# Output projection of three token tiles wholly in upper and lower parts, with three gate chunks converted later, on one Trainium2 core

## What is computed

```python
heads = concatenate([rms_norm(y_pool), rms_norm(y_attn), rms_norm(y_ssm)])
h = layer_norm(DN_ALPHA * x + heads @ w_out[i])
combine = route(h, w_router, router_bias)
ffn = moe(h, combine, ...)
ple = sigmoid(h @ w_ple_gate[i]) * (p[i] @ w_ple_proj[i])
x = layer_norm(DN_ALPHA * h + ffn + ple)
```

## Time and profile before

| | |
|---|---|
| time, median of 3 runs | 428.99 us (428.87 to 429.12) |
| time of the profiled execution | 429.05 us |
| its span, first to last instruction | 427.3 us |
| TensorE matmul busy | 413.3 us, 97% |
| TensorE weight load busy | 238.1 us, 56% |
| VectorE busy | 255.4 us, 60% |
| ScalarE busy | 129.6 us, 30% |
| GpSimd busy | 93.6 us, 22% |
| mean granted TensorE clock | 0.993 |

### The profile page before, as it was taken

The page is one execution under the profiler, slowest core; times in us unless marked ns, Lnnn a source line. Parts: engine busy times, 40 slices in busy tenths (PEclk is TensorE's granted clock), DMA queues, the critical chain, the costliest instruction groups (busy, mean ns, idle before and its releaser), DMA issues.

```text
span 427.3 us, 5594 instructions
## 1 busy us (share of the span) xinstructions
PE 413.3 (97%) x2167; PEld 238.1 (56%) x2167; DVE 255.4 (60%) x464; ACT 129.6 (30%) x235; POOL 93.6 (22%) x132
## 2 busy tenths in 40 slices
PE   8899999999999999999999999999999999999992
PEld 5677655469667555676577887333333433333271
DVE  2999985986873999998867524211101112224987
ACT  4721336025497890200621011011110111111243
POOL 2830269275000800000000742010111111000000
PEclk9999999999999999999999999999999999999997
DMA  7994103251997891111490428999999999977313
GB/s 264 431 397 129 49 2 66 68 130 51 276 411 295 285 392 63 49 49 51 158 384 8 191 43 325 425 410 413 418 417 418 421 411 411 423 289 247 152 45 153
DMA packets 33626, 102.76 MB, mean 240 GB/s; under 512 B 14882, under 2 KB 16082, under 8 KB 26816
## 3 DMA queue, kind: packets, MB, share of 16 engines
q1 hardware_dynamic: 26032, 92.79, 56.1%
q0 software_dynamic: 4016, 7.97, 5.6%
q10 hardware_dynamic: 3552, 1.65, 1.4%
HBM read 93.29 MB, written 15.24 MB: 254 GB/s over the span
## 4 chain that ended last, share of the span: by engine, by line
PE 67%; issue 23%; DVE 4%; DMA 3%; POOL 1%; ACT 1%; DVEq 0%; POOLq 0%; ACTq 0%
PE bank L1307 20%; PE bank L1317 10%; PE bank L952 7%; PE bank L1000 5%; PE bank L1302 3%; PE bank L967 3%; PE bank L992 3%; PE bank L1009 2%; PE bank L988 2%; PE bank L1067 2%; PE bank L1057 2%; POOL slot_scratch L595 1%; PE bank L995 1%; PE bank L1123 1%; PE bank L1122 1%
## 5 line engine op out<-in xcount | busy, mean ns | idle before, releaser
L1307 PE MATMUL bank<-region_a,region_g 128*64 128x512 f32 (+1 forms) x224 | 77.8, 594 | 0.0
L1317 PE MATMUL bank<-region_a,region_c 128*64 128x512 f32 (+1 forms) x160 | 43.7, 596 | 0.0
L1885 DVE TENSOR_TENSOR region_c<-region_c,bank 128x256 f32<-128x256 f32 x12 | 5.1, 421 | 64.6 <-ACT region_c L907 64.6
L1307 PE MATMUL bank<-region_h,region_g 128*64 128x512 f32 (+1 forms) x96 | 42.4, 594 | 0.0
L1307 PE MATMUL bank<-region_b,region_g 128*64 128x512 f32 (+1 forms) x96 | 42.4, 594 | 0.0
L1307 PE MATMUL bank<-region_c,region_g 128*32 128x512 f32 (+1 forms) x96 | 42.4, 594 | 0.0
L1878 DVE COPY region_g<-bank 128x512 f32<-128x512 f32 x24 | 15.5, 687 | 40.4 <-PE bank L1302 40.4
L1307 PEld LDWEIGHTS bank<-region_a,region_g 128*64 128x64 f32 (+1 forms) x224 | 22.2, 123 | 25.1 <-issue 24.4
L1151 PE MATMUL bank<-region_b,region_e 128*128 128x512 f32 x68 | 32.9, 607 | 0.0
L907 ACT ACTIVATE region_c<-bank 128x256 f32<-128x256 f32 x12 | 4.6, 384 | 83.9 <-PE bank L1307 83.9
L952 PE MATMUL bank<-region_e,region_a 128*128 128x512 f32 x64 | 28.0, 595 | 0.0
(11 more groups left out here) (364 smaller groups left out, 881.9 us busy)
## 6 DMA issues: line engine op xcount, KB each, us to landing
region_a<-in_w_exp_down SPq DMA_DIRECT2D x10, 1024.0 KB, 14.4
region_a<-in_w_exp_gate SPq DMA_DIRECT2D x7, 1024.0 KB, 8.4
region_a<-in_w_exp_up SPq DMA_DIRECT2D x7, 1024.0 KB, 12.1
region_b<-in_w_out SPq DMA_DIRECT2D x1, 4096.0 KB, 14.7
expert_scratch<-zero_scratch SPq DMA_DIRECT2D x8, 512.0 KB, 9.5
region_c<-in_w_ple_gate SPq DMA_DIRECT2D x2, 1536.0 KB, 23.1
region_b<-in_w_exp_gate SPq DMA_DIRECT2D x3, 1024.0 KB, 10.3
region_b<-in_w_exp_up SPq DMA_DIRECT2D x3, 1024.0 KB, 12.3
```

What stands on the lines that cost most here:

```text
L1307: return mm(out_[at:at + width].rearrange("p (u n) -> p u n", u=2), x[:, k, at:at + width], w[:, k], start=(k == 0), stop=(k == KD - 1), t ...
L1317: return mm(bank[banks[half]][at:at + width, :], act_e[:, r, 2, k * P + at:k * P + at + width], w[:, k, half * 512:half * 512 + 512], star ...
```

## The change

Tiles 1 to 3 of the output projection are multiplied in parts for all three groups. The upper parts of the heads' and weights' chunks 2, 3, 4 are made by ScalarE too (in new homes: among them the place of `pT`, and the place where the upper parts of gate chunks 4, 5, 6 will stand), the lower parts of the heads by VectorE, and the lower parts of weight chunks 2, 3, 4 by GpSimd, half by half, when tile 0 has read that half. The gate's chunks 7 and 3 are converted by ScalarE after the RMS square roots; chunks 4, 5, 6 (`PG_LAST`) by ScalarE once the last output product is done and ahead of the square root of tile 3, and by VectorE after `hidden_lower(3)` and ahead of the routing. `wo_read` goes up once per bank. `pT` is loaded after the last output product. A table load for the square root is placed by hand. The first gate products no longer wait for all chunks.

```diff
-WO_SPLIT = (5, 6, 7, 0, 1)
+WO_SPLIT = (5, 6, 7, 0, 1, 2, 3, 4)
-PG_FIRST, PG_ORDER = (0, 1, 2), (5, 6, 7, 4, 3)
+PG_FIRST, PG_NEXT, PG_LAST = (0, 1, 2), (7, 3), (4, 5, 6)
+PG_LATER = len(PG_NEXT + PG_LAST)
...
         wo_hi = {k: over(f"out_upper{k}", D, at) for k, at in
-                 ((0, A0), (1, A0 + 4 * D), (5, A0 + 4 * 2 * D), (6, A0 + 4 * 3 * D), (7, H0 + 4 * 6144))}
+                 ((0, A0), (1, A0 + 4 * D), (5, A0 + 4 * 2 * D), (6, A0 + 4 * 3 * D), (7, H0 + 4 * 6144),
+                  (2, A0 + 4 * 10240), (3, A0 + 4 * 11264), (4, A0 + 4 * 12288))}
...
+                  (2, H0 + 4 * 2048), (3, H0 + 4 * 2432), (4, H0 + 4 * 7168))}
...
             load(w_pp, io["w_ple_proj"].rearrange("(k p) n -> p k n", p=P), "wpp_in")
-            load(pT, io["pT"].rearrange("(k p) t -> p k t", p=P), "wpp_in")
...
                 sp.dma_start(h_d[t * P:(t + 1) * P, :], xh[:, t, :]).then_inc(S[f"h_out{t}"], 16)
 
             sp.wait_ge(S["pe_wo"], 2 * NT)
+            load(pT, io["pT"].rearrange("(k p) t -> p k t", p=P), "wpp_in")
             load_gu(0)
...
             add_squares(4, 2, 0)
+            for half in range(2):
+                cols = slice(half * 512, half * 512 + 512)
+                gp.wait_ge(S["wo_hi_set"], 16)
+                gp.wait_ge(S["pe_wo"], half + 1)
+                for k in MIX_AT[2]:
+                    g.tensor_tensor(wo_lo[k][:, cols], w_o[:, k, cols], wo_hi[k][:, cols], ALU.subtract).then_inc(S["gp_lo_set"], 1)
+            gp.wait_ge(S["pe_wo"], 2 * NT)
...
             for k in WO_SPLIT:
+                if k == 2:
+                    ac.wait_ge(S["pv_evac"], 3)
                 a.activation(hd_hi[k][:], hdT[:, k, P:T], ACT.Copy).then_inc(S["wo_hi_set"], 1)
             ac.wait_ge(S["wo_in"], 16)
-            for k in (0, 1, 5, 6, 7):
+            for k in (0, 1, 5, 6, 7, 2, 3, 4):
                 a.activation(wo_hi[k][:], w_o[:, k, :], ACT.Copy).then_inc(S["wo_hi_set"], 1)
...
-            ac.wait_ge(S["wpg_in"], 48)
-            for k in PG_ORDER[:4]:
-                gate_upper(k)
+            a.preload_act_table(ACT.Sqrt)
             ac.wait_ge(S["pe_sq"], 1)
...
+            ac.wait_ge(S["wpg_in"], 48)
             ac.wait_ge(S["sq_added"], 5)
-            gate_upper(PG_ORDER[4])
+            for k in PG_NEXT:
+                gate_upper(k)
...
             for t in range(NT):
+                if t == NT - 1:
+                    ac.wait_ge(S["pe_wo"], 2 * NT)
+                    for k in PG_LAST:
+                        gate_upper(k)
                 ac.wait_ge(S["z_ready"], t + 1)
...
                 for half in range(2):
-                    pe.wait_ge(S["wo_read"], 2 * t + half - 1)
-                    for group in range(2):
-                        if t == 1 and half == 0:
-                            pe.wait_ge(S["wo_hi_set"], (7, 10)[group])
-                            pe.wait_ge(S["wo_lo_set"], (7, 10)[group])
-                        mix_split(t, half, group)
-                    mix_part(t, half, 2).then_inc(S["pe_wo"], 1)
+                    for group in range(3):
+                        pe.wait_ge(S["wo_read"], 3 * (2 * t + half - 2) + group + 1)
+                        if t == 1:
+                            if group == 2:
+                                pe.wait_ge(S["wo_hi_set"], 16)
+                                pe.wait_ge(S["gp_lo_set"], 3 * half + 3)
+                            elif half == 0:
+                                pe.wait_ge(S["wo_hi_set"], (10, 13)[group])
+                                pe.wait_ge(S["wo_lo_set"], (10, 13)[group])
+                        last = mix_split(t, half, group)
+                    last.then_inc(S["pe_wo"], 1)
...
                 if half == 0:
-                    pe.wait_ge(S["ple_lo_set"], KD + t + 1)
+                    pe.wait_ge(S["ple_lo_set"], KD - len(PG_LAST) + t + 1)
+                elif t == 0:
+                    pe.wait_ge(S["ple_lo_set"], KD + NT)
...
+            ple_gate(0)
             pe.wait_ge(S["wpp_in"], 32)
-            ple_gate(0)
             ple_proj(0)
             turn_h(NT - 1)
...
                         last = stt(xh[:, t, cols], bank[WO_AT[half_][group]][:], rms_r[:, group, t:t + 1], xh[:, t, cols], ALU.mult, ALU.add)
-                        if group < 2:
-                            link(last)
-                    last.then_inc(S["wo_read"], 1)
-                    dv.wait_ge(S["wo_read"], 2 * t + half_ + 1)
+                        last.then_inc(S["wo_read"], 1)
+                        dv.wait_ge(S["wo_read"], 3 * (2 * t + half_) + group + 1)
...
                 if t == 0:
-                    gate_lower_of(1)
-                    gate_lower_of(2)
+                    dv.wait_ge(S["ple_hi_set"], 1)
+                    gate_lower(PG_NEXT[0])
                 elif t == 1:
-                    gate_lower_of(3)
                     hidden_lower(0)
                 elif t == 2:
-                    gate_lower_of(4)
+                    gate_lower(PG_NEXT[1])
             hidden_lower(1)
...
             hidden_lower(3)
+            for k in PG_LAST:
+                gate_lower(k)
```

More of the change, by code:

```diff
@@ L309, in trunk @@
             "kern_in kern_done rot_ready xrot_done "
-            "u_out u_back m0_in s_ready s_moved y_evac y_out y_back yin_ready gelu_done glu_lo_set glu_sig ssm_done "
+            "u_out u_back m0_in s_ready s_moved y_evac y_out gp_lo_set yin_ready gelu_done glu_lo_set glu_sig ssm_done "
             "pool_ready pool_mixed pe_u pe_qk pe_pool pe_v pe_bxT pe_kern pe_x pe_s pe_pt pe_pv pe_pm pe_y "
@@ L373, in _ @@
             for m in range(3):
-                load(yT[:, m, :].rearrange("p (j c) -> p j c", j=CH), y_d.rearrange("j f c -> f j c")[m * P:(m + 1) * P], "y_back")
+                load(yT[:, m, :].rearrange("p (j c) -> p j c", j=CH), y_d.rearrange("j f c -> f j c")[m * P:(m + 1) * P], "y_out")
             sp.wait_ge(S["rot_ready"], 3)
@@ L863, in _ @@
                     hidden_upper(0)
-            ac.wait_ge(S["pe_wo"], 2 * NT)
             hidden_upper(1)
@@ L875, in _ @@
             ac.wait_ge(S["ple_lo_set"], KD + NT)
+            ac.wait_ge(S["wpp_in"], 32)
             a.activation(p_hi[:], pT.rearrange("p k t -> p (k t)"), ACT.Copy).then_inc(S["ple_hi_set"], 1)
@@ L1161, in mix_split @@
                 for i, (x, w) in enumerate(terms):
-                    mm(bank[WO_AT[half][group]][:], x[:, (t - 1) * P:t * P], w[:, half * 512:half * 512 + 512],
-                       start=(i == 0), stop=(i == len(terms) - 1))
+                    last = mm(bank[WO_AT[half][group]][:], x[:, (t - 1) * P:t * P], w[:, half * 512:half * 512 + 512],
+                              start=(i == 0), stop=(i == len(terms) - 1))
+                return last
             def sum_squares(group, t):
@@ L1228, in ple_gate @@
                 else:
-                    pe.wait_ge(S["wo_read"], 2 * NT - 1 + k)
+                    pe.wait_ge(S["wo_read"], 3 * (2 * NT - 1 + k))
                 if half == 0:
-                    pe.wait_ge(S["ple_lo_set"], KD + t + 1)
+                    pe.wait_ge(S["ple_lo_set"], KD - len(PG_LAST) + t + 1)
+                elif t == 0:
+                    pe.wait_ge(S["ple_lo_set"], KD + NT)
                 for c in range(KD):
@@ L1249, in ple_proj @@
                     if k == NT:
-                        pe.wait_ge(S["ple_hi_set"], len(PG_ORDER) + NT + 2)
+                        pe.wait_ge(S["ple_hi_set"], PG_LATER + NT + 2)
                         pe.wait_ge(S["ple_lo_set"], KD + NT + 2)
@@ L1648, in _ @@
             row_max(5)
-            dv.wait_ge(S["y_back"], 48)
+            dv.wait_ge(S["y_out"], 96)
             for m in range(3):
@@ L1672, in gate_lower @@
                 tt(pg_lo[:, k * D:(k + 1) * D], pg_part[:, k, :], pg_hi[:, k * D:(k + 1) * D], ALU.subtract).then_inc(S["ple_lo_set"], 1)
-            def gate_lower_of(i):
-                dv.wait_ge(S["ple_hi_set"], i + 1)
-                gate_lower(PG_ORDER[i])
             def out_lower(k, i):
@@ L1690, in _ @@
             dv.wait_ge(S["pe_mix"], 1)
-            out_lower(0, 6)
-            out_lower(1, 7)
-            gate_lower_of(0)
+            out_lower(0, 9)
+            out_lower(1, 10)
             dv.wait_ge(S["pe_mix"], 2)
-            out_lower(5, 8)
-            out_lower(6, 9)
-            out_lower(7, 10)
+            out_lower(5, 11)
+            out_lower(6, 12)
+            out_lower(7, 13)
             dv.wait_ge(S["rms_sqrt"], 3)
@@ L1710, in hidden_lower @@
             def hidden_lower(t):
-                dv.wait_ge(S["ple_hi_set"], len(PG_ORDER) + t + 1)
+                dv.wait_ge(S["ple_hi_set"], t + (PG_LATER if t else len(PG_NEXT)) + 1)
                 tt(h_lo[t][:].rearrange("p (k t) -> p k t", k=KD), hT[:, :, t * P:(t + 1) * P],
@@ L1858, in _ @@
             link(v.tensor_copy(over_i[:, 0:1 + OVER], ov[0:1, :]))
-            dv.wait_ge(S["ple_hi_set"], len(PG_ORDER) + NT + 2)
```

(1 more changed line is left out.)

2 lines of the change are left out of this document (1 added, 1 removed).

## The result

| | before | after |
|---|---|---|
| time, median | 429.06 us (4 runs) | **434.1 us** (4 runs, 433.35 to 434.44) |
| ratio | | 1.0115, 95% interval 1.0103 to 1.0127 |
| time of the profiled execution | 429.05 us | 433.35 us |
| its span | 427.3 us | 431.5 us |
| TensorE matmul busy | 413.3 us, 97% | 411.3 us, 95% |

What follows compares the result with a forecast made beforehand. The prediction took TensorE, nearly gapless from the output projection to the experts, as the bound. Later `ple_proj(0)` +2.3, low clock +2.2 and subtractions +0.1 on 429.05 us, less 0.06, gave 433.5 us, range 430.7 to 435.3.

Steps and rivals of the forecast that it cites:

- TensorE's saving: Output projection: splitting group 2 saves 6 x 0.53 = 3.2 us, per-bank `wo_read` removes a 0.60 us wait; sum 3.8 us.
- Nothing holds TensorE back before it: Output projection: ScalarE's extra copies and GpSimd's subtractions, at 1.04 us each (1.92 beside VectorE), cost TensorE nothing.
- rival 2: Output projection: GpSimd subtractions over 2.0 us make TensorE wait at the first group 2 and slow VectorE; 435.5 us, chance 0.08.
- VectorE bounds the layer norm of tile 3: Tile loop: tile 3 begins at 194.3 without its TensorE wait; `h_ready` comes at 204.6, 3.5 us earlier.
- `pT` stands behind the store: SP's stream: `pT` issued at 205.0, landing 4.3 us later; TensorE waits 6.1 us, `ple_proj(0)` starts 2.3 us later.
- rival 3: Before `ple_proj(0)`: `pT` lands in time, so all 3.8 us stay and the kernel is faster; 425.2 us, chance 0.04.
- The clock: After TensorE's wait for `pT`: half clock for 4.4 us, costing 2.2 us (0 to 2.9).
- Rival 1: After `ple_gate(0)`: TensorE waits for `pT` but without the low clock; +2.4, 431.4 us, chance 0.20.
- Behind the stall: Ahead of the routing: three gate subtractions cost 0 to 0.4 us, taken as 0.1; the experts give no time back.
- The sum: Whole kernel: +2.3 + 2.2 + 0.1 = +4.6 on 429.05 us, less 0.06 to the median, giving 433.5 us.

## Why the prediction was right

**TensorE's saving** was given as 3.8 us (6 x 0.53 + 0.60). In the profiled execution `ple_gate(0)` starts 4.2 us earlier, at 197.23 where 197.6 was forecast. By the table above the split is worth 3.26 us (forecast 3.2) and the signals bank by bank 0.86: that term was too small, since it counted only the idle time in the row. It hardly moved the forecast, because TensorE then waits for `pT` in any case.

**Nothing holds TensorE back before it.** Right: no wait of TensorE from the output projection to 202.95. GpSimd's subtractions take 1.29 us, between the two bounds of 1.04 and 1.92; the trace before had a nearer row than either, a TENSOR_TENSOR of 128x512 (L580) at 138.48 with 1.27 us. VectorE's reads of the banks beside them still take 2.32 us for three. What the prediction only feared, a GpSimd at over 2.0 us for a subtraction, the slowed version shows: rival 2 had the mechanism and the place of the first wait, but was priced too low. It gave 2 us on top; that version, with a chunk ready every 2.6 us or more, lost 8.6, because the second wait, the clock behind both and the slowing of GpSimd itself had been left out. The Trainium skill ("SBUF — State Buffer", Who interferes with whom) says that a VectorE instruction with at most one SBUF input, outside the two-port modes, does not contend with GpSimd, and that one with two SBUF inputs contends with a GpSimd instruction that reads SBUF. The slowed version agrees on both sides: reads of a bank with one SBUF input stay at 2.32 us for three beside GpSimd, an addition with two SBUF inputs goes from 1.22 to 2.18.

**VectorE bounds the layer norm of tile 3.** Right: tile 3 begins at 194.27 (194.3), its wait for TensorE is gone, and `h_ready` comes at 204.54 (204.6). ScalarE, said to have little room before the square root of tile 3, was idle for 1.09 us before it.

**`pT` stands behind the store.** Right, and the heart of the result: issued at 204.95 (205.0), landing after 4.5 us. The forecast of 4.3 was the middle between two rows, 2.9 and 6.0, so that it came so close is partly luck. TensorE waits 6.53 us where 6.1 had been forecast, 0.25 of the difference because it came earlier, 0.2 because `pT` came later. That the store's place causes it, and not the size of the transfer or TensorE's need, is shown from both sides: `pT` moved out from behind the store gives 425.27 us where rival 3 had worked out 425.2 for a `pT` in time (with a saving of 3.8 reaching the end whole; in fact it was 4.15, of which 3.7 to 3.8 did), and `pT` put there alone makes the old kernel 8.2 us slower.

**The clock.** Taken as 2.2 us, for a low stretch of 4.4 us that was the middle of two marks. The profiled execution shows 3.0 us of it after the wait and a loss of about 1.6 (3.31 us for `ple_proj(0)` instead of 1.72). The median shows 2.2, as the difference to the version with the gap filled (434.1 - 431.86). Both hold: the profiled execution is the fastest of the four, 0.75 us below the median, with a mean granted clock of 0.988 where the other three have 0.985. That the clock would be low when TensorE resumed was reasoned from a row and came true. How long it would stay low was not: no row showed a return, the 4.4 us was the middle of two marks, and that it meets the median is luck. It stayed low for 3.0 us after the wait in the profiled execution and for 4.9 with only `pT` late. Rival 1, the wait without the low clock, would have been 431.4; the filled gap measured 431.86.

**Behind the stall.** The three gate subtractions stand ahead of the routing, from 216.77 to 220.3, where VectorE had idled before. They cost nothing there: the routing starts at 220.40, 7.61 us after `turn_h(3)`, as it did before (7.62). The delay of `turn_tokens`, 4.20 us, is still 0.1 above that of `turn_h(3)`, 4.10; it arises later in the routing chain and meets the 0.1 us of the prediction by luck. With `pT` early the subtractions do cost something: the routing starts 8.19 us after `turn_h(3)`. The expert part gives nothing back.

**The sum.** The terms add up to 433.59 us, which the prediction wrote as 433.5. In the profiled execution they measure 2.5 + 1.6 + 0.1 us against a forecast of 2.3 + 2.2 + 0.1, and the whole is 4.3 us longer; in the median it is 5.0, inside the range either way.

## What to carry to other kernels

When a load is moved to a later place in an engine's stream, compare the condition that it needs with the condition of what stands ahead of it: here the two were 8 us apart, and letting the load go ahead of the waiting store turned a loss of 5.0 us into a gain of 3.8. Price an idle stretch on TensorE with the clock behind it: waits of 1.85 to 6.5 us cost up to 2.4 us each on top, and in two runs with one of 3.2 us nothing. And a side job on GpSimd is free only as long as it ends before VectorE turns to operations that both slow down; here 0.3 us lay between the two. Compare executions from a common instruction: 0.4 us of difference between them hid half of what one part of the change was worth to TensorE.

## What the runs showed of the hardware beyond expectation

- **The clock lags behind the work in both directions.** It fell 2.75 us after TensorE's stop in the changed kernel, 3.8 us after it with only `pT` late, 3.0 us after the first stop with GpSimd slowed (stop at 165.56, fall at 168.6) and 4.5 us after it with the gap half filled (206.47 and 211.0). In the last two TensorE had been working again for 1.2 and 1.4 us when the clock fell. It was back 3.0, 4.9, 4.6 and 4.8 us after work had been taken up. A wait of 0.60 us, in the kernel before and with release per half, was followed by no fall.
- **Such a gap is a source of spread.** With the gap half filled the times fall into two pairs, 431.8 and 432.1 against 433.8 and 434.1; with the gap full they lie within 0.3 us, with it open within 1.1. That the pairs differ by the clock is seen in their mean granted clock, 0.995 against 0.989 and 0.991; why one run loses it and another does not stays open, since only the longer kind was profiled.
- **GpSimd is slowed about as much as VectorE.** Beside VectorE's layer norm a GpSimd subtraction of 128x512 went from 1.29 to 2.14 us, a VectorE addition of 128x1024 from 1.22 to 2.18.
- **A load between others lands later.** `pT`, 512 KB, landed after 3.8 us when issued alone and after 4.5 when issued 0.38 us behind a store of 512 KB, which itself landed after 3.0. Expert loads of 1024 KB followed it from 0.46 us on, so these runs do not say how much of the 0.7 us is due to the store.
